# Token projection with resident turned tokens, an S5 scan and a gated unit that work by channel

## The reference

```
hn = rmsnorm(x, norm_mix_w);  proj = hn @ w_in       # (T,1024) @ (1024,3600)
u, z, xbc, dt = proj[:1024], proj[1024:2048], proj[2048:3584], proj[3584:3600]

# S5, 64 groups of 16 channels, 64 complex states each
bu = B_bar . u ; h[t] = a * h[t-1] + bu[t] ; y = Re(C . h) + d * u
g = gelu(y);  y_s5 = rmsnorm(g * sigmoid(g @ w_glu), s5_norm_w)

# Mamba-2: convolution, chunked state space scan over tokens -> ym
y_m2 = grouped rmsnorm(ym * silu(z), m2_norm_w)

x = x + concat(y_s5, y_m2) @ w_out                   # (T,2048) @ (2048,1024)
x = x + peer_ffn(rmsnorm(x, norm_ffn_w))             # 8 heads, 16 experts per token and head
y = rmsnorm(x, final_norm_w)
```

## Time and profile before

| what | value |
|---|---|
| median of 3 runs | 4689.3 us (4685.39 to 4689.71) |
| the profiled execution | 4684.25 us, its span 4682.5 us |
| mean granted PE clock | 0.706 |
| PE busy | 2876.1 us (61%) |
| DVE busy | 2462.9 us (53%) |
| ACT / POOL busy | 1290.2 us (28%) / 1411.9 us (30%) |
| DMA | 1271.27 MB, mean 271 GB/s |

### The profile page before, as it was taken

The page is one execution under the profiler, slowest core; times in us unless marked ns, Lnnn a source line. Parts: engine busy times, 40 slices in busy tenths (PEclk is TensorE's granted clock), DMA queues, the critical chain, the costliest instruction groups (busy, mean ns, idle before and its releaser), DMA issues.

```text
span 4682.5 us, 54327 instructions
## 1 busy us (share of the span) xinstructions
PE 2876.1 (61%) x17688; PEld 1481.5 (32%) x17688; DVE 2462.9 (53%) x4924; ACT 1290.2 (28%) x3117; POOL 1411.9 (30%) x1547
## 2 busy tenths in 40 slices
PE   8999590745559995554654744645645546447444
PEld 5766460723334444221311411411312213114110
DVE  1000529248831113576576675674675765766754
ACT  1110020112222321333333333333333333333332
POOL 3000320301100000444444444444443444444443
PEclk9999755866779997665755755756757658658555
DMA  4111300121131112899999999999999999999998
GB/s 163 52 50 36 75 2 2 43 101 30 39 160 66 46 54 97 349 421 420 415 421 400 421 421 405 420 420 404 420 419 400 421 419 405 421 407 420 421 415 362
DMA packets 258478, 1271.27 MB, mean 271 GB/s; under 512 B 63984, under 2 KB 98672, under 8 KB 118128
## 3 DMA queue, kind: packets, MB, share of 16 engines
q0 software_dynamic: 156672, 1140.92, 58.8%
q1 hardware_dynamic: 101536, 127.12, 8.2%
HBM read 1225.69 MB, written 40.09 MB: 270 GB/s over the span
## 4 chain that ended last, share of the span: by engine, by line
DMA 40%; issue 7%; PE 6%; ACT 4%; DVE 4%; POOL 1%; POOLq 0%; SPq 0%; DVEq 0%; ACTq 0%
DMA pe_ring<-in_uv,pe_index_now 39%; PE pe_acc L1858 3%; DVE pe_ring L1781 2%; PE pe_ps_q L1831 2%; ACT pe_mark L1629 1%; ACT pe_weight L1631 1%; PE pe_ps_t L1851 1%; ACT L1629 1%; DVE pe_work_a L1662 1%; POOL pe_ring L1570 1%; ACT L1620 1%; DMA pe_w_q<-in_w_q 0%; DVE pe_pos L1714 0%; DVE pe_work_b L1715 0%; PE pe_ps_s L1841 0%
## 5 line engine op out<-in xcount | busy, mean ns | idle before, releaser
L1781 DVE CUSTOM_DVE_ANT_0 pe_ring<-pe_ring,pe_h_rep 128x1024 f32<-128x1024 f32 x1088 | 1330.7, 1226 | 961.3 <-DMA pe_ring<-in_uv,pe_index_now 881.3
L1858 PE MATMUL pe_acc<-pe_ring,pe_weight 128*32 128x256 f32 x8704 | 1018.5, 560 | 1232.3 <-ACT pe_weight L1631 1203.4
L1570 POOL DMA_INDIRECT pe_ring<-in_uv,pe_index_now x1088 | 1198.0, 1101 | 1471.2 <-PE pe_acc L1858 1275.3
L1858 PEld LDWEIGHTS pe_acc<-pe_ring,pe_weight 128*32 128x32 f32 x8704 | 210.8, 131 | 1973.1 <-ACT pe_weight L1631 1863.6
L1629 ACT ACTIVATE pe_mark<-pe_eye,pe_dot 128x32 f32<-128x32 f32 x1088 | 349.4, 321 | 1744.1 <-DVE pe_dot L1781 1690.3
L1631 ACT ACTIVATE pe_weight<-pe_mark,pe_gate_now 128x32 f32<-128x32 f32 x1088 | 349.5, 321 | 35.1
L1831 PE MATMUL pe_ps_q<-pe_h_t,pe_w_q 128*128 128x128 f32 x2304 | 329.5, 303 | 1.9 <-DMA pe_w_q<-in_w_q 1.9
L1831 PEld LDWEIGHTS pe_ps_q<-pe_h_t,pe_w_q 128*128 128x128 f32 x2304 | 302.7, 213 | 60.1 <-issue 57.8
L372 PE MATMUL pj_bank<-pj_w_in,pj_normed_t 128*128 128x512 f32 (+1 forms) x720 | 267.6, 529 | 5.7 <-DMA pj_w_in<-in_w_in 5.7
L1392 PE MATMUL mo_ps_out<-mo_w_out,mo_both_t 128*128 128x512 f32 x576 | 251.1, 594 | 14.8 <-DVE mo_both_t L1342 11.9
L378 PE MATMUL pj_bank<-pj_normed_t,pj_w_in 128*128 128x128 f32 x1728 | 195.2, 275 | 0.0
(11 more groups left out here) (312 smaller groups left out, 3222.6 us busy)
## 6 DMA issues: line engine op xcount, KB each, us to landing
pe_ring<-in_uv,pe_index_now POOLq DMA_INDIRECT x1088
pe_w_q<-in_w_q SPq DMA_DIRECT2D x4, 2048.0 KB, 18.3
m2s_window<-scratch_xbc SPq DMA_DIRECT2D x8, 786.0 KB
pj_w_in<-in_w_in SPq DMA_DIRECT2D x1, 6144.0 KB, 39.5
scratch_xbc<-pj_chan_out SPq DMA_DIRECT2D x8, 768.0 KB, 5.1
pj_x<-in_x_all SPq DMA_DIRECT2D x9, 512.0 KB
scratch_u<-pj_token_out SPq DMA_DIRECT2D x9, 512.0 KB, 2.6
scratch_z<-pj_token_out SPq DMA_DIRECT2D x9, 512.0 KB, 3.7
```

Of the source, the lines that this page charges most:

```text
L1570: nc.gpsimd.indirect_dma_start(out=ring[:, p, :], out_offset=None, in_=D["uv"], in_offset=bass.IndirectOffsetOnAxis(ap=row, axis=0)).then_ ...
L1781: V.tensor_tensor_reduce(out=ring[:, p, 0:D_MODEL], in0=ring[:, p, 0:D_MODEL], in1=h_rep[:, g % 2, :], scale=1.0, scalar=0.0, op0=ALU.mult ...
L1858: last = T.matmul(acc[j * PER:(j + 1) * PER, g % 2, 0:COLS], lhs(j), src[:, j * COLS:(j + 1) * COLS], start=first, stop=final)
```

## The change

Three of the five stages are written anew.

- The projection norms and turns all 9 tiles first and keeps them turned in `x_t`. The weights then stream through three slots of 256 columns each. u and xbc come out by channel: weights stationary, 512, 512 and 80 tokens moving; z and dt by token with 256 and 16 columns moving. The tokens that move for u are taken 8 apart, so that u lies in HBM ordered by step in the chunk, then chunk (`scratch_u_t`). The S5 tables are built in 16 steps on DVE between evictions, and the input weights are turned by PE in 8 groups (`turn_inputs`).
- The S5 stage has one block. u is loaded with (step, channel in group) on partitions, in two halves of 8 transfers, and needs no transpose. V matmuls come first, the chunk kernels and `toep` under the scan, and after the scan each pair gets its `toep` product and the products of its start states, which now contract over 64 rows each. ACT applies gelu and the result is stored by channel (`scratch_g_t`) in 4 batches of 8 transfers.
- The mix stage loads all of g by channel, works out the gated unit for all tokens in 3 parts of 368 by 8 blocks of channels, with the sum of squares as a matmul by ones (`add_sum`), and only then goes over the tiles for the output projection. `x` doubles as the residual and the result buffer; z, ym and x have one buffer each.

The diff, cut to its core:

```diff
+    pieces = []
+    for n, (kind, c) in enumerate(UNITS):
+        if n == U_UNITS:
+            pieces += [(n, "d", 0, t) for t in range(TILES)]
+        if kind == "z":
+            pieces += [(n, "z", c, t) for t in range(TILES)]
+        else:
+            pieces += [(n, kind, 2 * c + half, part) for half in range(2) for part in range(3)]
...
+            def weights(n):
+                if n >= WB:
+                    e = last_piece[n - WB]
+                    for v in (e - 1, e):
+                        sp.wait_ge(*made(v))
+                kind, c = UNITS[n]
+                a = FIRST_COL[kind] + c * CHUNK
+                sp.dma_start(w_buf[:, n % WB], D["w_in"][:, :, a:a + CHUNK]).then_inc(w_in[n % WB], 16)
...
+            for i in range(2, TILES):
+                sp.wait_ge(normed_ready, i - 1)
+                sp.dma_start(x[:, i % 2, :], D["x_all"][i * P:(i + 1) * P, :]).then_inc(x_in[i % 2], 16)
+                if i == 3:
+                    weights(1)
+            weights(2)
...
-                for j in range(ITEMS):
...
-                    if j < 5:
-                        a, w = j * 512, 512 if j < 4 else HEADS
-                        for k in range(KT):
-                            last = nc.tensor.matmul(b[:, 0:w], x_t[:, k, :], w_in[:, k, a:a + w],
-                                                    start=k == 0, stop=k == KT - 1)
...
+                if e < 3:
+                    pe.wait_ge(t_copied, TILES)
+                if e >= 4:
+                    pe.wait_ge(*taken(e - 4))
...
+                        last = T.matmul(b[:, 0:CHUNK], x_t[:, k, part * P:(part + 1) * P], w[:, k, :], start=first, stop=final)
...
+                        toks = x_t[:, k, SEQ:SEQ + REST] if part == 2 else x_t[:, k, part * 512:part * 512 + 512] if kind == "x" else x_t[:, k, 0:SEQ]
+                        if kind == "u":
+                            toks = toks.rearrange("p (k s) -> p s k", s=Q)
+                            toks = toks if part == 2 else toks[:, 4 * part:4 * part + 4, :]
+                        last = T.matmul(source(e, kind, part), lhs, toks, start=first, stop=final)
...
+                if e == 26 + 16 * (turned // 2) + 4 * (turned % 2) and turned < 8:
+                    turn_inputs(turned)
+                    turned += 1
...
+                if e == 9 + 4 * step and step < 16:
+                    table(step)
+                    step += 1
...
-            @block.sync
-            def _(sp):
-                with sp.Fori(0, PAIRS // 2) as r2:
-                    for j in range(2):
-                        r = 2 * r2 + j
-                        sp.wait_ge(u_turned, r + 1)
-                        for g in range(2):
-                            sp.dma_start(u_rest[:, j, g], rest_rows[:, :, bass.ds(r * G2 + g * S5_CH, S5_CH)]).then_inc(rest_in[j], 16)
...
+            by_step = D["u_t"].rearrange("(g c) s k -> s c g k", c=S5_CH)
+            part = lambda n: slice(n * S5_GROUPS // HALVES, (n + 1) * S5_GROUPS // HALVES)
+            for n in range(HALVES):
+                for s in range(Q):
+                    sp.dma_start(u_t[s * S5_CH:(s + 1) * S5_CH, part(n), :], by_step[s, :, part(n), :]).then_inc(u_in[n], 16)
...
+            out_by_step = D["g_t"].rearrange("(g c) s k -> s c g k", c=S5_CH)
+            for n in range(PAIRS // BATCH):
+                sp.wait_ge(y_kept, (n + 1) * BATCH)
+                groups = slice(2 * n * BATCH, 2 * (n + 1) * BATCH)
+                for s in range(Q):
+                    sp.dma_start(out_by_step[s, :, groups, :], u_t[s * S5_CH:(s + 1) * S5_CH, groups, :]).then_inc(g_out, 16)
+            sp.wait_ge(g_out, 16 * Q * PAIRS // BATCH)
...
+                for h in range(2):
+                    for g in range(2):
+                        last = T.matmul(two(bank[g * 64:g * 64 + 64, r % 4], CHUNKS)[:, h, :], in_t[:, r, h, g * 64:g * 64 + 64],
+                                        u_t[:, 2 * r + g, :], start=True, stop=True)
+                last.then_inc(v_made, 1)
...
+            pe.wait_ge(scanned, 1)
+            for r in range(PAIRS):
+                if r >= 4:
+                    pe.wait_ge(y_kept, r - 3)
+                y = [bank[:, 2 * (r % 4) + g, 0:CHUNKS] for g in range(2)]
+                for g in range(2):
+                    T.matmul(y[g], toep[:, 2 * r + g, :], u_t[:, 2 * r + g, :], start=True, stop=False)
+                for h in range(2):
+                    for g in range(2):
+                        rows = slice(g * 64, g * 64 + 64)
+                        T.matmul(y[g][:, CH_REST:], out_w[rows, r, h, S5_CH:], state[rows, r, h, CH_REST - 1:CHUNKS - 1], start=False, stop=False)
+                    for g in range(2):
+                        rows = slice(g * 64, g * 64 + 64)
+                        last = T.matmul(y[g][:, 0:CH_REST], out_w[rows, r, h, S5_CH:], rest_start[rows, r, h, :], start=False, stop=h == 1)
+                last.then_inc(y_made, 1)
...
-            with sp.Fori(0, MAIN_TILES) as k:
-                sp.wait_ge(m2_gated, k + 1)
-                sp.wait_ge(g_ready, k + 1)
-                load_y(k + 1)
-                store(k)
+            for k in range(TILES):
+                if k < MAIN_TILES:
+                    sp.wait_ge(m2_turned, k + 1)
+                    load(k + 1)
+                sp.wait_ge(x_mid_ready, k + 1)
+                sp.dma_start(D["x_mid"][k * P:(k + 1) * P, :], x[:]).then_inc(x_mid_out, 16)
+                if k < MAIN_TILES:
+                    sp.wait_ge(x_mid_out, 16 * k + 16)
+                    sp.dma_start(x[:], D["x_all"][(k + 1) * P:(k + 2) * P, :]).then_inc(x_in, 16)
...
+            norm_m2(0)
+            weigh_m2(0)
+            for n in range(PARTS):
+                if n:
+                    dve.wait_ge(s5_ready, KT * n)
+                for c in range(KT):
+                    dve.wait_ge(sig_ready, KT * n + c + 1)
+                    if n == 0 and c == 0:
+                        dve.wait_ge(g_in, 16 * KT)
+                    V.tensor_tensor(out=by_step(s5_raw[:, c, :]), in0=cut(g_t, c, n), in1=by_step(sig[:, c % 2, :]), op=ALU.mult).then_inc(s5_made, 1)
+                dve.wait_ge(r_root, n + 1)
+                chain.link(V.reciprocal(r_b[:], r_b[:]))
+                for c in range(KT):
+                    V.scalar_tensor_tensor(out=s5_t[:, c, n * N:(n + 1) * N].rearrange("p (k s) -> p s k", s=Q), in0=by_step(s5_raw[:, c, :]),
+                                           scalar=norm_w[:, c:c + 1], in1=by_step(r_b[:]),
+                                           op0=ALU.mult, op1=ALU.mult).then_inc(s5_ready, 1)
+            dve.wait_ge(s5_ready, KT * PARTS)
+            for k in range(TILES):
+                if k < MAIN_TILES:
                     norm_m2(k + 1)
+                    weigh_m2(k + 1)
                 dve.wait_ge(out_made, k + 1)
                 dve.wait_ge(x_in, 16 * k + 16)
+                V.tensor_tensor(out=x[:], in0=x[:], in1=ps_out[:].rearrange("p b c -> p (b c)"), op=ALU.add).then_inc(x_mid_ready, 1)
...
+            def turn(k):
+                pe.wait_ge(m2_ready, k + 1)
+                if k:
+                    pe.wait_ge(m2_t_ready, k)
...
+            for n in range(PARTS):
+                for c in range(KT):
+                    C = KT * n + c
+                    if C >= 2:
+                        pe.wait_ge(sig_ready, C - 1)
+                    for kk in range(KT):
+                        last = T.matmul(by_step(ps_glu[:, c % 2, 0:N]), w_glu[:, kk, c * P:(c + 1) * P], cut(g_t, kk, n),
+                                        start=kk == 0, stop=kk == KT - 1)
+                    last.then_inc(glu_made, 1)
+                    if C == 0:
+                        turn(0)
+                    if C:
+                        add_sum(C - 1)
+            add_sum(PARTS * KT - 1)
...
+            for k in range(TILES):
+                if k < MAIN_TILES:
+                    turn(k + 1)
                 pe.wait_ge(m2_t_ready, k + 1)
+                if k:
+                    pe.wait_ge(x_mid_ready, k)
+                toks = slice(REST + k * P, REST + (k + 1) * P) if k < MAIN_TILES else slice(0, P)
+                for b in range(2):
+                    cols = slice(b * 512, b * 512 + 512)
+                    for c in range(KT):
+                        T.matmul(ps_out[:, b, :], m2_t[k % 2][:, c, :], w_out[:, KT + c, cols], start=c == 0, stop=False)
+                if k == 0:
+                    pe.wait_ge(s5_ready, KT * PARTS)
+                for b in range(2):
+                    cols = slice(b * 512, b * 512 + 512)
+                    for c in range(KT):
+                        last = T.matmul(ps_out[:, b, :], s5_t[:, c, toks], w_out[:, c, cols],
+                                        start=False, stop=c == KT - 1)
+                last.then_inc(out_made, 1)
```

More of the change, by code:

```diff
@@ L284, in _ @@
[L284 to L287 removed]
+            A(tmp[:, 7, :], tmp[:, 6, :], ACT.Sin).then_inc(act_done, 1)
+            kept = 0
```

(23 more changed lines are left out.)

999 lines of the change are left out of this document (414 added, 585 removed).

## The result

The changed kernel takes 4837.1 us in the median of 4 runs (4835.34 to 4839.17), the kernel before 4688.2 (4685.39 to 4689.71): a ratio of 1.0319, with a 95% interval from 1.0301 to 1.0336. The forecast was 4720, and rival B 4830. The profiled execution took 4839.17 us with a span of 4837.4.

What follows compares the result with a forecast made beforehand. No one engine bounds the three changed stages, though PE's matmuls bound the projection. Projection +28, S5 -176 and mix +179 give +31 on the profiled 4684.25, so 4715; the median stands 5 higher: 4720, range 4660 to 4845.

Steps and rivals of the forecast that it cites:

- rival B: Projection: u's moving reads of one fp32 in eight slow PE, +109 us, kernel at 4830; 33 in 100.
- u's matmuls: Projection: u and xbc take 273.3 us for 640 instructions of 512 columns, 36.2 for 320 of 80.
- Projection start: Projection: all nine tiles normed and turned first, so the first matmul starts near 55.5 us, not 19.0: +36.
- dt and turns: Projection: 144 dt instructions take 16.7 us, 64 program transposes of the input weights 7.2 us.
- S5: S5 stage: 447.2 to 271 us, -176, summed as 61.5 + 120 + 75.6 + 14.
- Two of the bounds: S5 output: 64-row matmuls going side by side, -30 us; output at half clock after the long scan, +70.
- rival C: S5 output: matmuls over 64 rows overlap, 16 a pair cost 8, -30 us, kernel at 4690; 19 in 100.
- Mix: Mix stage: 440.4 to 620 us, +179, summed as 22.9 + 157 + 48.2 + 357 + 29 + 5.
- The largest term: Mix output, tiles 1 to 7: PE waits for store, loads and norm; 51.1 us a tile, 357 in all.
- Rival D: Mix output: tiles do not wait for z and ym; kernel about 4605, or 4570 if nothing shows; 8 in 100.
- Mamba: Mamba stage: keeps code, data and order, so its change was counted at nothing.
- the sign: Whole kernel: slower than before, 71 in 100; same 12, faster 17.

Runs made afterwards that it cites:

- e1: Changed kernel with u's matmuls reading tokens packed and the eviction placing them by step and chunk; 4707.2 us, ratio to before 1.0043.
- e7: Changed kernel with the nine dt pieces each put behind a piece of the last z unit; 4818.9 us.
- e9: Changed kernel with 400 unused full-row matmuls of 138 columns on PE ahead of the S5 output; 4794.4 us, median of two executions.
- e5: Changed kernel with three buffers each for the mix stage's x, z and ym, loaded two to four tiles ahead; 4765.1 us.
- e6: Kernel of e5 with PE turning tile k+1 after tile k's first 16 matmuls and two alternating PSUM places; 4682.2 us, ratio to before 0.9994.
- e2: Changed kernel with u's channel blocks reading tokens at different distances (1, 2, two of 8, 4, 8, 16); 4796.0 us, one run.

## Why the prediction was wrong, step by step

- **u's matmuls.** The step that failed is the one that valued them "640 instructions of 512 columns, 273.3 us", with u's reads as fast as xbc's, and so kept rival B out of the sum. The term measured 405.5, and 283.7 counted the same way with packed reads (e1). B had the place, the mechanism and nearly the price: +109 to +114 forecast, +130 measured (e1), since one element out of 16 bytes costs more than twice packed: 0.919 us against 0.429, or 2.14, not 2.0. The 80-column ones went from 0.109 to 0.147. The argument that PE takes only one element in 0.83 ns and could stand it was the wrong one to follow: the earlier trace rows had shown 1.96 ns an element on DVE at a 40 byte stride, and PE's 1.79 ns lies close to it. The packed price was read with a slip that did no harm: in the earlier trace rows 208 instructions are transposes and dt (2512 less 1728 and 576), not 272, which makes a 512-column one 0.430 us and not 0.417; packed, it measured 0.429.
- **Projection start.** 45.0 us and not 55.5. A tile took 4.1 us in the steady run and not 5.14: from the third tile on ACT did squares and roots in turn with no table load between them (none from 16.81 to 38.71), where the row had one before each in the first tile. -10.
- **dt and turns.** 16.7 forecast, 29.6 measured, +13, and the turns +3: the clock fell in a run of busy work. I had costed the clock only where PE stood idle. e7 gives back dt's 12.9 and 1.8 of the turns.
- **S5.** The loads came as forecast: the first V matmul at +23.3 us (forecast 23.5), the second half at +43.8 (45). V itself was quicker, 0.6 us a pair (16 pairs in 9.56 us at a mean clock of 0.80) and not 0.95, so the scan began at +53.9 and not 61.5; from there to the output 122.1 and not 120; the end 10.9 and not 14. The output took 97.1 and not 75.6. Two of the bounds came true at once, and one took off part of the other: the half rows do run side by side (rival C; 3.01 us a pair at half clock, where 20 at 0.23 would be 4.6), and the clock stayed at half. The clock's cost is what e9 gives back, 43 us; that C saved the other way is luck in a sum that had neither.
- **Mix.** The largest term was right in every link and 7% too long: 47.9 us a tile against 51.1. Rival D is wrong, and e5 and e6 show the two waits that it denied. The part up to the first tile's end was 226 us against 228.1, and right in its pieces too: 23.8 to the first matmul (22.9), 156.5 of gated unit (157), 45.7 of tile 0 (48.2).
- **Mamba.** +3 us with the same code. The stage took 409.8 to 414.3 us over the twelve kernels traced, 410.2 and 414.0 in e1 and e2, which differ from the changed kernel in u's matmuls and evictions alone; so this is scatter of that stage and no cost of the change. What moves it isn't settled.

So the sign was right, and e1 shows it right for the reasons given, since it holds without u's term (+20 us). The size was wrong for one reason: +31 forecast, +149 measured, 130 of it in one access pattern.
